# mLSTM heads on VectorE: scores leave their bank ahead of the previous head's output operations, and head 2's output projection is split around the last norm sum

## What is computed

```python
def mlstm_layer(h, w_in, conv_w, conv_b, wq, wk, wv, w_if, b_if, gn_g, skip, w_out):
    xm, z = jnp.split(h @ w_in, 2, axis=-1)
    xc = jax.nn.silu(causal_conv(xm, conv_w, conv_b))
    q = jnp.einsum('bshd,hde->bhse', xc_h, wq)
    k = jnp.einsum('bshd,hde->bhse', xc_h, wk) * (DH ** -0.5)
    v = jnp.einsum('bshd,hde->bhse', xm_h, wv)
    gates = jnp.transpose((xc @ w_if + b_if), (0, 2, 1))
    ...
        s = jnp.einsum('bhtd,bhsd->bhts', qc, kc) * w_intra
        num = jnp.einsum('bhts,bhsd->bhtd', s, vc) + ...
        den = s.sum(-1) + ...
        h = num / jnp.maximum(jnp.abs(den), jnp.exp(-m_t))[..., None]
    ...
    mu = hh.mean(-1, keepdims=True)
    var = jnp.square(hh - mu).mean(-1, keepdims=True)
    hh = (hh - mu) * lax.rsqrt(var + LN_EPS)
    hh = hh.transpose(0, 2, 1, 3).reshape(B, S, MLSTM_INNER) * gn_g
    hh = (hh + skip * xc) * jax.nn.silu(z)
    return hh @ w_out
```

## Time and profile before

| | |
|---|---|
| median of three runs | 2435.8 us (2435.09 to 2443.53) |
| the profiled execution, own time | 2435.83 us |
| its span in the trace | 2434.0 us |
| TensorE busy | 2276.6 us, 94% of the span |
| VectorE busy | 1247.4 us, 51% |
| ScalarE busy | 950.9 us, 39% |
| mean granted TensorE clock | 0.978 of full speed |

### The profile page before, as it was taken

The page is one execution under the profiler, slowest core; times in us unless marked ns, Lnnn a source line. Parts: engine busy times, 40 slices in busy tenths (PEclk is TensorE's granted clock), DMA queues, the critical chain, the costliest instruction groups (busy, mean ns, idle before and its releaser), DMA issues.

```text
span 2434.0 us, 33290 instructions
## 1 busy us (share of the span) xinstructions
PE 2276.6 (94%) x12894; PEld 1743.6 (72%) x12894; DVE 1247.4 (51%) x2278; ACT 950.9 (39%) x1702; POOL 113.8 (5%) x96
## 2 busy tenths in 40 slices
PE   5999998998899899969999899999999999899999
PEld 4877774454477444448878679888888886698887
DVE  4624534111323511147763666677677636666776
ACT  2532202111222211145544665654454446645543
POOL 1000000000000000000005200000000052000000
PEclk9999999999999999989999999999999999899999
DMA  9975439999721899946653415466566525054663
GB/s 355 321 235 206 156 135 406 429 429 425 283 104 70 369 428 430 427 132 188 196 189 114 166 45 199 120 208 191 155 195 194 193 95 183 26 184 139 204 185 95
DMA packets 310256, 535.68 MB, mean 220 GB/s; under 512 B 14894, under 2 KB 200944, under 8 KB 296304
## 3 DMA queue, kind: packets, MB, share of 16 engines
q1 hardware_dynamic: 309180, 532.61, 60.7%
q10 hardware_dynamic: 948, 1.28, 0.2%
HBM read 532.81 MB, written 1.05 MB: 219 GB/s over the span
## 4 chain that ended last, share of the span: by engine, by line
PE 83%; DVE 8%; ACT 3%; DMA 3%; issue 2%; SPq 1%; ACTq 0%; DVEq 0%
PE bank L593 15%; PE bank L1046 14%; PE bank L875 13%; PE yacc L909 9%; PE bank L880 7%; PE bank L577 4%; PE yacc L788 2%; PE yacc L610 2%; PE bank L628 2%; PE bank L1264 1%; PE bank L657 1%; PE yacc L1058 1%; PE bank L986 1%; PE yacc L1208 1%; PE bank L750 1%
## 5 line engine op out<-in xcount | busy, mean ns | idle before, releaser
L1428 ACT ACTIVATE arena<-bank 128x256 f32<-128x256 f32 (+3 forms) x382 | 146.7, 407 | 585.6 <-PE bank L593 126.8
L875 PE MATMUL bank<-h_split,w_hi 128*128 128x512 f32 x1408 | 352.3, 392 | 0.0
L2321 DVE TENSOR_TENSOR w_lo<-wring,w_hi 128x1024 fp32r<-128x1024 f32 x264 | 307.3, 1218 | 10.7 <-ACT w_hi L1649 10.7
L1649 ACT ACTIVATE w_hi<-wring 128x1024 fp32r<-128x1024 f32 x264 | 277.5, 1056 | 49.0 <-PE yacc L909 49.0
L875 PEld LDWEIGHTS bank<-h_split,w_hi 128*128 128x128 f32 x1408 | 259.3, 189 | 50.0
L880 PEld LDWEIGHTS bank<-h_split,w_lo 128*128 128x128 f32 x1408 | 193.4, 191 | 20.4 <-DVE h_split L2363 5.5
L880 PE MATMUL bank<-h_split,w_lo 128*128 128x256 f32 x1408 | 199.5, 284 | 5.3 <-DVE h_split L2363 5.3
L2900 POOL TENSOR_TENSOR wx_lo<-wring,wx_hi 128x1024 fp32r<-128x1024 f32 x42 | 107.3, 2557 | 1947.5 <-ACT wx_hi L1468 1947.5
L1046 PE MATMUL bank<-wring,arena 128*64 128x512 f32 x768 | 172.3, 603 | 15.8 <-issue 8.3
L1046 PE MATMUL bank<-arena 128*64 128x512 f32 x672 | 169.7, 599 | 10.1 <-issue 6.3
L1661 ACT ACTIVATE H<-bank 128x256 f32<-128x256 f32 x176 | 67.4, 383 | 252.4 <-PE bank L880 250.5
(11 more groups left out here) (403 smaller groups left out, 3814.6 us busy)
## 6 DMA issues: line engine op xcount, KB each, us to landing
wring<-in_ffn_w_in SPq DMA_DIRECT2D x176, 512.0 KB
wring<-in_w_ada SPq DMA_DIRECT2D x28, 2048.0 KB
wring<-in_ffn_w_out SPq DMA_DIRECT2D x88, 512.0 KB
wring<-in_w_in SPq DMA_DIRECT2D x20, 2048.0 KB
wring<-in_moe_w_gate SPq DMA_DIRECT2D x16, 2048.0 KB, 21.5
wring<-in_moe_w_up SPq DMA_DIRECT2D x16, 2048.0 KB, 21.2
wring<-in_moe_w_down SPq DMA_DIRECT2D x16, 2048.0 KB, 22.6
arena<-in_moe_w_down SPq DMA_DIRECT2D x12, 2048.0 KB, 20.2
```

The source lines that it names most:

```text
L875: return mm(b[:, :], r(w_hi[:, j % 2, g, c * HB:(c + 1) * HB]), r(h_split[:, c, :, :].rearrange("p a t -> p (a t)")), start=start, stop=st ...
L1428: ins = f(dst, bank_of(name)[0:dst.shape[0], 0:T] if src is None else src, func, **kw)
L1649: f(w_hi[:, j % 2, part, :].bitcast(F32R), wring[:, u % WSLOTS, part * DC * HB:(part + 1) * DC * HB], ACT.Copy).then_inc(w_hi_ready[part], 1)
L2321: tt(w_lo[:, j % 2, part, :].bitcast(F32R), wring[:, (u0 + j) % WSLOTS, part * DC * HB:(part + 1) * DC * HB], w_hi[:, j % 2, part, :], ALU ...
```

## The change

On VectorE `mlstm_out` is cut in two. The first half, now `mlstm_scaled(h-1)`, stays ahead of head h's weights. The second half, still called `mlstm_out(h-1)`, moves behind head h's scores. For the last head both follow each other as before. On TensorE `head_out` takes a range of output tiles. Head 2's tiles 0 to 2 are computed between `mlstm_mean(3)` and `mlstm_var(3)`, its tiles 3 to 7 behind `mlstm_var(3)`. No instruction is added or removed, except that a piece's slot is now looked up by its tag.

```diff
-            def head_out(h):
-
-                w = weights(f"a_w_out{h}")[:, 0:DHC * D].rearrange("p (k n) -> p k n", k=DHC)
-                pe.wait_ge(head_ready.sem, head_ready.upto("pe"))
-                for m in range(DC):
+            def head_out(h, first=0, end=DC):
+
+                if first == 0:
+                    weights(f"a_w_out{h}")
+                    pe.wait_ge(head_ready.sem, head_ready.upto("pe"))
+                u = tags.index(f"a_w_out{h}")
+                w = wring[:, u % WSLOTS, 0:DHC * D].rearrange("p (k n) -> p k n", k=DHC)
+                for m in range(first, end):
...
-                freed[-1] = y0_summed, (DC // 2) * (h + 1)
+                freed[u] = y0_summed, (DC // 2) * (h + 1)
 
             head_out(0)
             mlstm_num(NH - 1)
             head_out(1)
             mlstm_mean(NH - 1)
+            head_out(2, 0, 3)
             mlstm_var(NH - 1)
-            for h in range(2, NH):
-                head_out(h)
+            head_out(2, 3)
+            head_out(3)
...
-            def mlstm_out(h):
+            def mlstm_scaled(h):
 
                 dve.wait_ge(*drained(f"gvar{h}"))
                 link(v.reciprocal(nrm[:, 0, :], nrm[:, 0, :]))
                 link(tt(hm, hm, rows(nrm[:, 0, :], DHC), ALU.mult))
+
+            def mlstm_out(h):
                 c = DHC * h
...
                 if h > 0:
-                    mlstm_out(h - 1)
+                    mlstm_scaled(h - 1)
...
                 moved(f"mS{h}", stt(Pm[h % 2][:, 1, P:T], b[:, T + P:2 * T], DH ** -0.5, W[:, 1, P:T], ALU.mult, ALU.mult))
+                if h > 0:
+                    mlstm_out(h - 1)
             mlstm_num(NH - 1)
+            mlstm_scaled(NH - 1)
             mlstm_out(NH - 1)
```

## The result

| | before | after |
|---|---|---|
| median | 2435.8 us | 2425.0 us |
| range, 8 runs each | 2435.1 to 2443.5 | 2417.2 to 2431.2 |
| ratio | | 0.994, 95% interval 0.9924 to 0.9955 |
| profiled execution, own time | 2435.83 us | 2427.64 us |
| its span | 2434.0 us | 2425.8 us |

The account below looks back on a forecast made before the run. TensorE, busy for 94% of the span, was taken as the bound, so gains come from its idle time or lower-clock products. 2.67 + 4.59 + 7.5 = 14.8 us off 2435.8 gave 2421.0 us, range 2414 to 2429.

Parts of the forecast that it names:

- The q products' waits: TensorE's waits for VectorE's score operation in heads 2 and 3 vanish, gaining 2.67 and 4.59 us.
- The moved operations cost nothing: VectorE's output operations, run behind the scores, fit its idle time; tightest slack 1.4 us, ahead of head 2's denominator.
- The last norm sum: Twelve products fill TensorE's gap before this sum; up to the projection's end 28.28 instead of 35.77 us, gaining 7.5.
- The cover ahead of `head_out(3)`: Head 3's output is ready at 336.11 us and TensorE asks at 337.04, 0.9 us to spare.
- The stream moves forward as a whole: Experts' loads, queued behind conditioning loads issued as each `head_out` ends, start earlier, so the 7.5 us gain is kept.
- the time behind the stage: Execution after `head_out(3)`: taken as unchanged, with a spread of two clock falls either way, 5 us.
- The first rival: Later waits: two more clock falls there eat the 4.8 us won from lower clock; 2425.8 us, chance 0.16.
- every sign of the stage in place: No score waits, q products some 7.1 us, full clock from 190 us, no `head_out(3)` wait, 28.3 us, earlier load issue.
- the clock's part: Share of the gain from products no longer at lower clock, behind head 3's wait and the norm sum: 2.06 + 2.7 = 4.8 us.
- another release: ScalarE's conditioning copy or the mask bank still holds the q products; only 7.5 us come, 2428.3 us, chance 0.07.
- a stream that gives nothing back: Experts' weights land at the same time as now, so the wait at L1046 grows; 2435.8 us, chance 0.03.
- a slower kernel: TensorE's waits behind 400 us lose the full clock, at 2.7 us each at most; 2450 us, chance 0.03.

Follow-up runs that it names:

- the second trace: The changed kernel run and traced once more with no edit; its span was 2418.0 us, 7.8 less than in the first profiled execution.
- The useless products: Changed kernel plus products whose result nobody reads (3, 4 and 6) in three idle TensorE stretches ahead of both layers' experts; 2424.3 us.
- the padded kernel: Changed kernel plus 34 products that nobody reads after `head_out(2)` and `head_out(3)`'s split point, putting later stages back to about their old times; median 2434.9 us.

## Why the prediction was right, and where its size was off

- **The q products' waits.** Right in place, cause and size. Head 2's products take 7.17 instead of 9.84 us, a gain of 2.67 (forecast 2.67). Head 3's take 7.17 instead of 11.66, a gain of 4.49 (forecast 4.59).
- **The moved operations cost nothing.** Right. Their cover was measured at 1.48 us (forecast 1.4).
- **The last norm sum.** Right. From 314.12 us, where the mean's sum ends, to 342.18 TensorE takes 28.1 us (forecast 28.3), and the granted clock is 1.00 in every one-microsecond window from 190 us on. The gain is 7.7 us (forecast 7.5). The cover ahead of `head_out(3)` was 0.8 us, and one tile more turned it into a wait of 0.94 us.
- **The stream moves forward as a whole.** Right. The last load of the conditioning is issued at 342.2 us, against 358.6 and the 343.8 forecast; 1.5 of the 16.4 us is the lead with which this execution entered the stage. The chain of the changed kernel shows the wait for the experts as before:

```profile
353.06 27.29 DMA wring<-in_moe_w_gate
380.34 0.24 issue
380.58 16.92 PE bank L1050 x64
```

  From the end of the projection to the first expert product it is 380.58 - 342.18 = 38.4 us, against 38.9 before. The wait itself is 2.8 us instead of the some 4 forecast, since the products ahead of it met a fall of the clock.
- **The step that was off: the time behind the stage.** The sum took it as unchanged, with two falls of the clock more or fewer as its spread. It was 4 us longer by the medians of the eight runs, 8.2 in the profiled execution and 0.2 in the second trace. By the means of all runs it is under 2 us, which is not clear of nothing. The forecast started from 2435.8 us, which belongs to the lower of the old kernel's two groups of times. The first rival forecast what the eight runs gave: a gain near 10 us with every sign of the stage in place, because later falls eat as much as the clock's part. Its 2425.8 us lie nearer to the measured 2425.0 than the forecast does, and its mechanism is what the first trace shows. The second trace is the forecast's case. The stage itself gained its full 14.9 us, 4.8 of clock among them, in all three traces of this kernel. So the stage was understood, and where in the range the total fell was up to falls that nobody could place. Their cause stays open.
- **The other rivals** (another release, a stream that gives nothing back, a slower kernel) found nothing in the traces.

## What to carry to other kernels

Give a bank back before doing work on the same engine that nobody waits for yet, and put independent products into the gap of a chain that goes through other engines. The timelines of such a stage give the gain to 0.1 us, and the slack of each cover says how much further the split can go. What can't be had to better than some us is everything behind: two executions of the same kernel differed by 8 us there through the clock's falls alone. So compare stages in the traces when a change is worth 0.5%, and take means of many runs of both kernels before a missing us is explained. And before filling idle time to hold the clock, see who sets the pace there: here it was worth nothing while the DMA engines were busy for 0.99 of the time, and little behind VectorE and ScalarE.

## What the runs showed that was not expected

- The same wait of 2.40 us kept the clock in one trace and lost it in another, at a cost of 1.6 us.
- In three traces the clock also fell where TensorE was busy without a break, toward the end of 32 records of products only 32 columns wide (in the first of them 4.24 us instead of 3.65, and 2.06 instead of 1.21 for the eight records behind).
- The useless products, 0.437 us each, held the granted clock at 1.00 through 25 us in which it was 0.73 without them.
- The kernel before has two groups of times in its runs, near 2435 and near 2441 us (14 of 45 are above 2440), while the padded kernel, with the same later stages at the same times, has only the first. The cause stays open.
